# Down stage of a decoder trunk: activation loads from the third block on issued by ScalarE, and three smaller changes of order

## The reference

```python
h = h + jnp.concatenate([y_conv, y_ret], axis=-1) @ w_out
hn2 = rmsnorm(h, norm_mlp)
h = h + jnp.square(jax.nn.relu(hn2 @ w_up)) @ w_down   # D 1024 -> 4096 -> 1024
...
y_prompt = rmsnorm(hp, norm_final)[:, N_META:]
y_sample = rmsnorm(hs, norm_final)
```

## Time and profile before

| what | value |
|---|---|
| three runs | 1165.01, 1164.90, 1163.75 us, median 1164.9 |
| the profiled execution | 1164.33 us |
| its span, first to last instruction | 1162.5 us |
| TensorE busy | 1143.7 us (98%) |
| VectorE, ScalarE, GpSimd busy | 764.1, 432.9, 554.9 us (66%, 37%, 48%) |
| granted TensorE clock, mean | 0.996 |
| up stage, down stage in TensorE's list | about 484 to 814, 814 to 1150 us |
| activation loads in the down stage | 56 of 516 KB, all on SP's queue |

### The profile page before, as it was taken

How to read it: one execution, slowest core, us unless ns; L and a number is a source line. 1 busy time by engine, 2 the same in 40 slices (tenths; PEclk the granted TensorE clock), 3 DMA queues, 4 the chain that set the end, 5 groups by cost and what they waited for, 6 DMA issues and landing times.

```text
span 1162.5 us, 22545 instructions
## 1 busy us (share of the span) xinstructions
PE 1143.7 (98%) x8689; PEld 1119.7 (96%) x8689; DVE 764.1 (66%) x1143; ACT 432.9 (37%) x859; POOL 554.9 (48%) x541
## 2 busy tenths in 40 slices
PE   9999999999999999998999999999999999999996
PEld 7899999999999999998999999999999999999996
DVE  4345446456355675787777777777877767777756
ACT  6423313214124433543333333334544444544414
POOL 0154243253150330143233242322989999998992
PEclk9999999999999999999999999999999999999999
DMA  6431211211301232253534435346864544454213
GB/s 203 133 111 37 76 54 54 74 54 40 88 19 58 58 108 92 72 167 109 183 119 147 146 124 178 110 145 230 280 204 129 183 153 143 136 187 136 87 38 146
DMA packets 153992, 139.79 MB, mean 120 GB/s; under 512 B 6794, under 2 KB 118131, under 8 KB 153901
## 3 DMA queue, kind: packets, MB, share of 16 engines
q1 hardware_dynamic: 148799, 135.50, 36.4%
q10 hardware_dynamic: 5102, 3.05, 0.9%
HBM read 98.07 MB, written 40.47 MB: 119 GB/s over the span
## 4 chain that ended last, share of the span: by engine, by line
PE 83%; POOL 10%; DVE 3%; issue 1%; DMA 1%; ACT 1%; SPq 0%; POOLq 0%; ACTq 0%; DVEq 0%
PE pair L1867 14%; PE pair L1868 14%; PE pair L1869 14%; PE pair L1668 8%; PE pair L1670 8%; PE pair L1669 8%; POOL dn_lo L772 7%; PE pair L1844 3%; PE pair L1846 3%; PE pair L1845 3%; PE pair L1710 1%; PE pair L1711 1%; PE pair L1713 1%; POOL dn_s L762 1%; POOL dn_s L760 1%
## 5 line engine op out<-in xcount | busy, mean ns | idle before, releaser
L1867 PE MATMUL pair<-m_hi,dn_hi 128*128 128x258 f32 (+2 forms) x896 | 255.6, 285 | 3.6 <-DVE a L1639 2.3
L1867 PE MATMUL pair<-b_hi,up_hi 128*128 128x258 f32 x896 | 255.7, 285 | 3.0 <-DVE hid L1515 3.0
L1868 PE MATMUL pair<-b_lo,up_hi 128*128 128x258 f32 x896 | 254.3, 284 | 0.0
L1868 PE MATMUL pair<-m_lo,dn_hi 128*128 128x258 f32 (+2 forms) x896 | 253.6, 283 | 0.0
L1869 PE MATMUL pair<-m_hi,dn_lo 128*128 128x258 f32 (+2 forms) x896 | 253.4, 283 | 0.0
L1869 PE MATMUL pair<-b_hi,up_lo 128*128 128x258 f32 x896 | 252.9, 282 | 0.0
L1668 PE MATMUL pair<-x_hi,w_both 128*128 128x344 f32 (+2 forms) x576 | 188.6, 328 | 0.0
L1670 PE MATMUL pair<-x_hi,w_both 128*128 128x344 f32 (+2 forms) x576 | 184.3, 320 | 0.0
L1669 PE MATMUL pair<-x_lo,w_both 128*128 128x344 f32 (+2 forms) x576 | 184.2, 320 | 0.0
L1639 DVE TENSOR_TENSOR hid<-pair,hid 128x516 f32<-128x516 f32 (+2 forms) x194 | 124.6, 642 | 77.3 <-PE pair L1869 75.7
L1867 PEld LDWEIGHTS pair<-b_hi,up_hi 128*128 128x128 f32 x896 | 169.9, 190 | 5.2 <-DVE up_lo L1431 3.2
(11 more groups left out here) (209 smaller groups left out, 2147.6 us busy)
## 6 DMA issues: line engine op xcount, KB each, us to landing
m_raw<-m_dram SPq DMA_DIRECT2D x56, 516.0 KB, 4.8
m_dram<-hid SPq DMA_DIRECT2D x64, 258.0 KB, 2.6
up_raw<-w_up_dram SPq DMA_DIRECT2D x32, 512.0 KB, 5.1
dn_raw<-w_down_dram SPq DMA_DIRECT2D x128, 128.0 KB, 2.4
w_raw<-w_in_dram SPq DMA_DIRECT2D x28, 512.0 KB, 3.7
m_dram<-hid SPq DMA_DIRECT2D x16, 774.0 KB, 3.9
h_dram<-hid SPq DMA_DIRECT2D x8, 516.0 KB, 3.3
h_in<-h_dram SPq DMA_DIRECT2D x16, 258.0 KB, 4.3
```

The costliest lines, as they stand in the source:

```text
L1867: m_.matmul(to, shs[k], mhs[k], start=STARTS[i] and k == 0, stop=False, skip_group_check=more)
L1868: m_.matmul(to, shs[k], mls[k], start=False, stop=False, skip_group_check=more)
```

## The change

Four edits of order. No operation is added or removed, apart from one multiply that was two halves and is one whole.

1. SP issues `load_h(0, 0..3)` ahead of `store_row(LASTU, 6)` and `store_row(LASTU, 2)`; on ScalarE `mid_split(6)` moves from the last product of the up stage to behind the copy of a1 in the first down unit.
2. The 42 loads of blocks 2 to 7 are issued by ScalarE (`act_load_mid`) at the heads of the first three units of blocks 1 to 6 (three, two and two of them); SP keeps those of blocks 0 and 1.
3. `mid_sum(1, 0..3)` stand in unit 2 as those of unit 0 do in unit 1: behind the reads, two at i = 1, two at i = 2.
4. `final_norm(4)` is split into its reciprocal, behind product 5 of the last unit, and its multiply, behind the last read and the sum for group 5 (`first_sums`).

```diff
-           (NW + 2, 2): (3, 0), (NW + 2, 3): (3, 1), (NW + 2, 5): (4, 0), (NW + 2, 6): (4, 1)}
+           (NW + 2, 2): (3, 0), (NW + 2, 3): (3, 1), (NW + 2, 5): (4, 2)}
...
             load_down(1)
-            store_row(LASTU, 6)
-            store_row(LASTU, 2)
             for n in range(KT):
                 sp.wait_ge(h_saved[n], 16)
             for i in range(4):
                 load_h(0, i)
+            store_row(LASTU, 6)
+            store_row(LASTU, 2)
             load_mid(7)
             load_mid(8)
+            def load_mids(wi):
+
+                b, n = wi // 4, wi % 4
+                for j in ((2,), (3, 4), (5, 6), ())[n]:
+                    load_mid(7 * (b + 1) + j)
+
...
-                if b < BLOCKS - 1:
-                    for j in ((2,), (3, 4), (5, 6), ())[n] if b == 0 else ((0, 1, 2), (3, 4), (5, 6), ())[n]:
-                        load_mid(7 * (b + 1) + j)
+                if b == 0:
+                    load_mids(wi)
...
-                        for j in ((), (0,), (1,), (2,), (3,), (4, 5), (6,))[i]:
+                        for j in ((), (0,), (1,), (2,), (3,), (4, 5), ())[i]:
                             mid_split(j)
                         down_split(0, i)
...
+            def act_load_mid(m):
+
+                b, j = m // 7, m % 7
+                for i in range(2):
+                    act.wait_ge(first_saved[i], stores(2 * b + 2, i))
+                    act.wait_ge(c22_saved[i], stores(2 * b + 2, i))
+                    act.wait_ge(c21_saved[i], stores(2 * b + 2, i))
+                    act.wait_ge(rest_saved[i], 2 * stores(2 * b + 2, i))
+                act.wait_ge(mid_high, m - 6)
+                act.wait_ge(dn_done, 28 * (b - 1))
+                act.dma_start(m_raw[b % 2][j][:, :, :], m_dram[2 * b:2 * b + 2, :, j, :].rearrange("u p c -> p u c")).then_inc(mid_in[j], 16)
+
             for q, (b, n, ts) in enumerate(DN):
+                if 0 < b < BLOCKS - 1:
+                    for j in ((0, 1, 2), (3, 4), (5, 6), ())[n]:
+                        act_load_mid(7 * (b + 1) + j)
...
                         s.activation(a1[:, n, :].rearrange("p (t c) -> p t c", c=TQ), pair[BANK[0]][:, :, 0:TQ], ACT.Copy).then_inc(a1_copied, 1)
+                    if q == 0 and i == 0:
+                        mid_split(6)
...
-                    if i == 0 and q > 1:
+                    if i == 0 and q > 2:
                         for j in range(4):
                             mid_sum(q - 1, j)
...
-                    if q == 1 and i in (1, 2):
-                        mid_sum(0, 2 * i - 2)
-                        mid_sum(0, 2 * i - 1)
+                    if q in (1, 2) and i in (1, 2):
+                        mid_sum(q - 1, 2 * i - 2)
+                        mid_sum(q - 1, 2 * i - 1)
...
-                if part != 1:
+                if part in (None, 0, 2):
                     dve.wait_ge(fstd_done, i + 1)
...
-                if part is None:
+                if part in (None, 3):
...
-                else:
+                elif part < 2:
...
             first_sums()
+            final_norm(REST, 3)
             for i in range(FIRST_LATE, len(FINAL)):
                 final_norm(i)
```

## The result

The changed kernel takes 1157.86 us (median of four runs, 1157.13 to 1158.05), the kernel before 1164.95 (1163.75 to 1165.16): 7.1 us less, a ratio of 0.9943 with a 95% interval of 0.9928 to 0.9958. The profiled execution took 1157.13 us, its span 1155.3 where it was 1162.5. The forecast was 1156.6, in 1154.4 to 1160.4.

A forecast was written before the change was run, and what follows sets the result against it. TensorE, 98% busy, was taken as the bound, so order could win only its waits. Terms 4.0 + 1.4 + 1.15 + 1.05 + 0.4 = 8.0 us, off 1164.33 or 1164.9, gave 1156.6 us, range 1154.4 to 1160.4.

The forecast's parts named there:

- sums of unit 1: Up unit 2: TensorE's wait on L1515 and the slow clock go, a 0.67 us wait before product 5 comes; net 4.0 us.
- start of the down stage: Down unit 0: h_in lands before its read and the copy of a1 runs earlier; net 1.4 us won, bounds 0.9 and 1.64.
- loads, unit 5: Down unit 5: block 2's loads issued earlier by ScalarE, so TensorE's late start goes; 1.15 us won (0.9 to 1.25).
- unit 13: Down unit 13: GpSimd's lead over TensorE grows, mid_split(28) comes 1.35 us earlier in relation; 1.05 of 1.44 us won.
- the end: Last read: without the rest rows' norm ahead of it, it runs at about 1150.5; 0.4 us won, bounds 0 and 0.5.
- 1.54 us of slow clock: Up unit 2: cost of the lowered clock behind TensorE's stall, 18 matmuls in 3.70 us; part of the place's 4.70 us.
- GpSimd 0.5 us earlier from split (0,6): Start of the down stage: the earlier split puts GpSimd 0.5 us ahead, counted besides 3.4 us in its lead at unit 13.
- rival (a): Down units 0, 5 and 13: GpSimd becomes the bound, only 1.5 us remain instead of 3.6; 1158.7 us, chance 12%.
- (b): Up unit 2 only moves its wait: L1522 over 3 us late, clock down again, 4.0 us lost; 1160.6 us, chance 6%.
- (c): ScalarE's loads land late, 8.2 us instead of 4.8, sharing engines with SP's weight loads; 1159.7 us, twice 1162.8; chance 7%.
- (d): Slower than before: ScalarE held at the loads, 2.5 us each, 2 us lost at each of 12 heads; 1181 us, 4%.
- (e): Whole kernel: the edits act but waits hidden by the profile fill their gains; time within 0.2%, chance 4%.

## Why the prediction was right

| step | forecast | by the profile |
|---|---|---|
| sums of unit 1 | 4.0 | 4.1 (up stage 332.0 to 327.9) |
| start of the down stage | 1.4 | 1.0 |
| loads, unit 5 | 1.15 | 1.3 |
| loads, unit 9 | 0 | 0.2 |
| unit 13 | 1.05 | 0.7 |
| the end | 0.4 | 0.3 |
| sum | 8.0 | 7.6, less 0.4 that the untouched stages took longer |

Timed, the gain is 7.1 us by the medians and 6.6 by the ratio; the four edits alone add up to 7.1 us by their ratios, so nothing large is left between them. The measured 1157.86 lies 1.3 us above the forecast, inside its range. That the profiles came as near as 7.6 to 8.0 is in part luck: the start and unit 13 were counted 0.75 us too high, units 5 and 9 0.35 too low.

*Sums.* Right in place and order; the wait that would come next was named with its length (0.67 forecast, 0.65 measured). What I took for a fixed price, 1.54 us of slow clock, is one value of three (0, 1.4, 2.8). The forecast rested on a single profile, and was lucky that it had the middle one.

*Start.* Mechanism right: the read did lack h_in. But the reason that I gave does not fit it: issued at 816.44 and landing after 4.3 us, h_in would have come at 820.7, behind the read of 819.43; by the trace it landed at 819.33, after 2.9. The term is mis-sized by 0.4: VectorE's m_lo took 0.99 us each beside GpSimd. And "GpSimd 0.5 us earlier from split (0,6)" was wrong in sign: GpSimd's first low of unit 1 came 8.00 us behind TensorE's first matmul of unit 0, where it was 7.39. Beside VectorE's m_lo its lows took 1.27 and 1.19 us instead of 0.7, so an earlier split did not make it faster. And for the edit alone the gain of unit 0 was mostly given back by unit 14, which the forecast did not count.

*Loads.* Right, and shown apart: the order does it (units 5 and 9 lose their waits, and GpSimd is some 4 us earlier at unit 6, with SP issuing early too), and the same early place on SP costs more in the later blocks than it wins. The 1.3 us of unit 5 is one pair of profiles: over units 3 and 5 together, kernels with the old place lose 0.4 to 1.6 us and those with the early one 0.0 to 0.6. The price of 0.7 us a load and the free time of ScalarE held; twice the issues changed nothing that could be measured.

*Unit 13.* Mechanism right, mis-sized by 0.35: GpSimd's lead over TensorE grew by 0.7 us instead of 1.35, since at unit 13 GpSimd was 3.2 us earlier instead of 3.9. With the loads alone, where TensorE isn't sped up ahead of it, the wait is gone altogether. This is not rival (a), in which TensorE waits for GpSimd's lows: with GpSimd as late and one m_lo moved behind the read, the wait is gone as well. What is left is a chain from GpSimd's sums over m_hi and m_lo to the read, and VectorE's order is a link of it.

*The end.* 0.29: the read could start 0.48 behind the last matmul, and I had counted 0.4 off a modelled end.

*The rivals.* (b) and (c) did not occur: the clock stayed full from 530 to 545 us (1.00), the longest landing of these loads was 6.3. (d) did not occur either, and its price was misworked: at 2.5 us a load only the six heads of three loads pass 5.5 us, not twelve. (e) holds for the first edit alone. What makes the sixth tile of block 1 land 5.7 us behind unit 3's start in one profile and 7.6 in another was not tried. Where unit 3 waits, unit 5 waits less or not at all: with the old place of the loads, 0.0 and 1.3 us (before), 0.5 and 1.1, 0.6 and 0.4, 0.4 and 0.0, 1.5 and 0.0. So single profiles of the same down stage differ by up to 0.9 us (sums of 4.4 to 5.3).

## What to carry to other kernels

Before moving a transfer to another engine's queue, ask what stands ahead of it on the present one: the gain here was the wait of another engine's work that it had been queued behind, and giving it the same early place on the old queue made the kernel slower, because its own wait then held back what followed. An operation that only feeds a later stage belongs behind the read for which TensorE waits, but follow it to its last user: the sums were harmless late in thirteen units and cost 9 us (up stages of 333.7 and 324.9) in the one whose store stood ahead of the next stage's loads. When a gain comes from making the bound engine earlier, check that the engine which feeds it becomes earlier too: unit 0's 1.0 us came to little alone, because TensorE's start of unit 14 followed GpSimd's first low of unit 13 by 18.0 us in every such kernel.

## What the runs showed of the hardware that was not expected

TensorE's granted clock after one and the same wait of 3.0 us at one and the same place was full in one execution (on another chip than three of the others), half for 3.4 us in others and half for 6.8 us in one (mean 1.00, 0.89 and 0.77 over 15 us), worth 0, 1.4 and 2.8 us. It also fell behind a wait of 1.8 us, and stayed full behind waits of 1.3 us, and one of 1.6, in the down stage. A wait of this size has a price that one profile does not show.
